# Dealing the weight products out among the attention slots: half a tile to a slot, or a whole tile to every second one

## What is computed

```
p  = project(modulate(rms_norm(x)), mix_w_in)
ya = diff_attend(...)       # 8 heads, two score maps each, p0 - lam * p1
yb = sink_attend(...)       # 16 query heads, window of 128 tokens, sink column
yc = mla_attend(...)        # 8 heads, scores from two parts (128 + 64 wide)
merged = ga * (ya @ branch_w[0]) + gb * (yb @ branch_w[1]) + gc * (yc @ branch_w[2])
```

## Time and profile before

| | us |
|---|---|
| median of three runs | 2768.34 |
| the runs | 2767.23 to 2771.36 |
| span of the profiled execution (one more execution) | 2769.1 |
| TensorE busy in it | 2694.7 (97%) |
| TensorE weight loads | 2257.3 (82%) |
| VectorE busy | 1745.0 (63%) |
| ScalarE busy | 1240.7 (45%) |
| GpSimd busy | 220.3 (8%) |

### The profile page before, as it was taken

One profiled execution on the slowest core, in us unless ns is written; L12 is line 12 of the kernel. 1 busy time (PEld: TensorE's weight loads), 2 busy tenths in 40 slices (PEclk: granted clock), 3 DMA queues, 4 the chain that ended last, 5 costly groups with the idle time before them and its releaser, 6 DMA issues.

```text
span 2769.1 us, 42026 instructions
## 1 busy us (share of the span) xinstructions
PE 2694.7 (97%) x15406; PEld 2257.3 (82%) x15406; DVE 1745.0 (63%) x2891; ACT 1240.7 (45%) x2212; POOL 220.3 (8%) x302
## 2 busy tenths in 40 slices
PE   8999999999999999999999999999999999998998
PEld 6888898886766776788888898888988777877996
DVE  6777366657755443358676385773667886646764
ACT  3222355227655444445222353222553576554543
POOL 0011010110100000010000000010102110000000
PEclk8999999999999999999999999999999999999999
DMA  7555357431111221145455455553555322424654
GB/s 277 181 188 194 102 163 242 130 106 39 47 46 39 73 91 39 54 160 184 160 195 163 119 174 183 189 193 109 157 189 175 122 77 70 127 83 152 230 179 152
DMA packets 105634, 384.42 MB, mean 139 GB/s; under 512 B 12049, under 2 KB 12321, under 8 KB 103569
## 3 DMA queue, kind: packets, MB, share of 16 engines
q1 hardware_dynamic: 85250, 303.34, 33.9%
q0 software_dynamic: 20240, 79.14, 8.8%
HBM read 379.27 MB, written 3.16 MB: 138 GB/s over the span
## 4 chain that ended last, share of the span: by engine, by line
PE 87%; DVE 8%; ACT 3%; DMA 1%; issue 1%; POOL 0%; SPq 0%; DVEq 0%; ACTq 0%; POOLq 0%
PE ps L2186 23%; PE ps L2194 22%; PE ps L2187 22%; PE ps L956 4%; PE ps L935 3%; PE ps L918 2%; DVE wlo L1613 2%; PE ps L2250 1%; PE ps L908 1%; PE ps L2252 1%; PE ps L2247 1%; PE ps L2126 1%; PE ps L2277 1%; PE ps L2274 1%; PE ps L2278 1%
## 5 line engine op out<-in xcount | busy, mean ns | idle before, releaser
L1613 DVE TENSOR_TENSOR wlo<-raw,whi 128x1024 fp32r<-128x1024 f32 x570 | 695.9, 1229 | 414.4 <-ACT whi L1233 413.3
L1233 ACT ACTIVATE whi<-raw 128x1024 fp32r<-128x1024 f32 x570 | 603.1, 1058 | 503.4 <-PE ps L2194 411.8
L2186 PE MATMUL ps<-xhi,whi 128*128 128x512 f32 (+1 forms) x2432 | 819.6, 351 | 6.5 <-DVE xlo L1804 5.3
L2187 PE MATMUL ps<-xlo,whi 128*128 128x512 f32 (+1 forms) x2432 | 812.1, 348 | 0.0
L2186 PEld LDWEIGHTS ps<-xhi,whi 128*128 128x128 f32 x2432 | 461.3, 190 | 71.0 <-DVE xlo L1804 6.5
L2187 PEld LDWEIGHTS ps<-xlo,whi 128*128 128x128 f32 x2432 | 461.6, 190 | 57.1
L2194 PE MATMUL ps<-xhi,wlo 128*128 128x512 f32 (+1 forms) x2432 | 505.1, 350 | 2.7 <-DVE wlo L1613 2.7
L2194 PEld LDWEIGHTS ps<-xhi,wlo 128*128 128x128 f32 x2432 | 399.2, 190 | 60.6 <-DVE wlo L1613 3.3
L1943 DVE SCALAR_TENSOR_TENSOR work<-ada,work 128x1024 f32<-128x1024 f32 x256 | 299.6, 1221 | 5.9 <-DMA ada<-in_ada_rows 5.9
L806 DVE TENSOR_REDUCE mx<-ps 128x2 f32<-128x1024 f32 (+1 forms) x120 | 125.2, 1045 | 185.6 <-PE ps L914 81.5
L2186 PE MATMUL ps<-ghi,whi 128*128 128x256 f32 (+1 forms) x792 | 233.5, 320 | 0.1
(11 more groups left out here) (253 smaller groups left out, 3438.7 us busy)
## 6 DMA issues: line engine op xcount, KB each, us to landing
raw<-in_ffn_in SPq DMA_DIRECT2D x192, 512.0 KB, 4.8
ada<-in_ada_rows POOLq DMA_DIRECT2D x128, 512.0 KB, 4.0
raw<-in_merge SPq DMA_DIRECT2D x96, 512.0 KB, 3.5
raw<-in_ffn_out SPq DMA_DIRECT2D x72, 512.0 KB, 3.6
raw<-in_v_a SPq DMA_DIRECT2D x32, 512.0 KB, 4.3
raw<-in_qk_a SPq DMA_DIRECT2D x32, 512.0 KB, 3.5
raw<-in_ffn_out SPq DMA_DIRECT2D x36, 384.0 KB, 3.2
raw<-in_out_rows SPq DMA_DIRECT2D x22, 512.0 KB, 3.5
```

The lines of the kernel that those rows point to most:

```text
L1233: act.activation(whi[:, g.ring(SPLIT), :], raw[:, g.ring(RAW), :], ACT.Copy).then_inc(hi_ready, 1)
L1613: dve.tensor_tensor(wlo[:, g.ring(SPLIT), :], raw[:, g.ring(RAW), :], whi[:, g.ring(SPLIT), :].bitcast(F32), ALU.subtract).then_inc(lo_rea ...
L2186: pe.matmul(o, w, hi[:, first + c, ph.span], start=start, stop=False)
L2187: pe.matmul(o, w, lo[:, first + c, ph.span], start=False, stop=False)
```

## The change

`share` rounds each cumulative number of ticks down to an even one. A slot then gets no product step or two, and a tile's high and low half stand in one slot, on TensorE, ScalarE, VectorE and GpSimd alike. Nothing is computed otherwise, no instruction is added or removed, and the number of ticks of a phase stays the same.

```diff
     parts = [3] + [1] * (2 * ph.steps)
     whole, so_far, out = sum(parts), 0, []
+    assert ticks % 2 == 0
     for part in parts:
         so_far += part
-        out.append(so_far * ticks // whole)
+        out.append(so_far * ticks // whole // 2 * 2)
     return out
```

## The result

The changed kernel takes 2800.74 us, the median of four runs (2797.33 to 2804.88), against 2768.16 (2767.23 to 2771.36) for the kernel before beside it: a ratio of 1.0113, 95% interval 1.0101 to 1.0125, 31 us slower. The forecast was 2792, in a range of 2774 to 2808. The profiled execution has a span of 2797.2 us. Lines of the changed kernel stand one further down: L935 is now L936, L918 is L919, L1233 is L1234.

What follows compares the result with a forecast made beforehand. TensorE, busy 97% of the span, was the engine to follow, with only 20.5 us of waits in the attentions. Terms 11.2 + 5.7 + 10 + 1.6 - 4.7 = +23.8 us gave 2792, range 2774 to 2808.

Steps and rivals of the forecast that it cites:

- The bound, and the place: Six attention windows, 690.8 us with 20.5 of waits: their sum grows by 24, and nothing moves outside them.
- Term 1: Attention starts: high halves that covered the first chain move away, leaving TensorE waiting; +11.2 us, bounds 8 and 12.
- Term 4: Starts of a0 and a1: idling about 3.0 us lowers TensorE's granted clock; one such cost, +1.6 us, bounds 0 and 5.
- Term 2: Modes b and c: steps left without product work make TensorE wait; +5.7 us, bounds 2 and 10.
- Term 3: Mode a: VectorE falls behind in longer stretches without products; +7 us in a0 and +3 in a1.
- Term 5: Attention units: 59 fewer entries into product work save 0.08 us each; -4.7 us, bounds -1.8 and -11.8.
- Nothing measurable: Rival: VectorE's leads cover mode a's stretches, starts cost 8, switches save 8; +5 us, 2773; chance 0.12.
- Faster by switches: Rival: each of 59 saved entries is worth 0.3 us, 17.7 in all; -5.7 us, 2762.6; chance 0.05.
- The others being the bound: Rival: ScalarE and VectorE bound the attentions, 41 added steps without products cost 0.7 each; +42 us, 2810; chance 0.12.

Runs made afterwards that it cites:

- starts kept: The changed kernel, but slots 0 to 3 of each attention keep the old list, whole tiles from slot 4 on: 2779.35 us, ratio 1.0037 to the kernel before.
- waits filled: The changed kernel with extra matmuls, results unused, in TensorE's waits at four attention starts (a0, b0, a1, b1): 2790.44 us, ratio 1.0079 to the kernel before.
- run 7: The changed kernel, with ScalarE, VectorE and GpSimd doing each tile's second step one slot later than TensorE, except latnorm's sums: 2805.45 us, ratio 1.0132.
- run 5: The kernel before, with only TensorE walking the new list (except latnorm's two sums), the other engines the old one: 2807.27 us, ratio 1.0148.
- run 2: The kernel before, but slots 0 to 3 of each attention have the new list, the old one behind: 2787.64 us, ratio 1.0070.
- run 11: The kernel before with extra matmuls, results unused, in two TensorE waits outside the attentions (8.9 and 3.0 us): 2766.20 us, ratio 0.9994.

## Why the prediction was right, step by step

**The bound, and the place.** Right: the six windows grew by 28.2 where 24 was forecast, and what moved outside them adds up to nothing.

**Term 1, the starts: +11.2.** Right in place and size. All waits stand where they were put: 3.0 us in a0, 0.9 grown to 3.0 in a1, 1.9 in b0, 1.0 grown to 2.9 in b1. The kernel after lies 21.0 above the run with its starts kept; less the 9.4 of the filled waits that is 11.6, give or take 5. The stages say it more finely: waits filled less starts kept is 3.1, 2.6, 1.2, 2.0 and 2.0 in a0, b0, c0, a1 and b1, where 3.6, 2.7, 0.8, 2.0 and 2.1 were forecast.

**Term 4, the clock: +1.6.** This is the term that was mis-sized. The step that failed is "I take one such cost": the same pause stands at every start that loses its half, and the text said itself that a0 and a1 would both idle for 3.0 us. The clock fell behind four starts, twice as long in a0, 8.5 us of lost clock in the profile, of which filling the waits returned 9.4 (give or take 5) in the medians and 5.9 in the touched stages. By the stages the stated bound of 5 was too low as well. Its other half, that slow matmuls partly fill waits, holds in part: 2.9 of 5.1 us of lost clock were paid in a0 and b0, 3.0 of 3.4 in a1 and b1.

**Term 2, steps in modes b and c: +5.7.** Right. With the starts kept, the windows of b0, c0, b1 and c1 hold 2.7, 0.8, 0.8 and 0.8 us more of waits than before, 5.1.

**Term 3, mode a: +10.** Half as large, and for another reason. With the starts kept a0 and a1 hold 2.8 and 2.7 more, 5.5. For a0 that is 0.2 us to each of 14 tiles, where 0.5 was forecast and below 0.2 was to count as a sign of being wrong. A lag of VectorE's would show as turns waiting for `prob` from VectorE, or as ScalarE waiting for maxima ahead of the scores' wait. The first fell in a0, from 1.1 to 0.7; the second is in neither of the two longer waits of scores behind a0's start (run 7). What grew is the scores behind ScalarE's `prob` (1.5 us in a0), the turns behind `back` (0.7 in a0, 1.1 in a1) and those behind GpSimd's scaling (0.6 and 0.4). Ahead of these scores stand ScalarE's copies of the tile, which the prediction had declared harmless. What delays `back` and the scaling was not taken apart by a run.

**Term 5, switches: -4.7.** Wrong. An entry's 0.11 us is in the record of the low half, but in sum TensorE's busy time moved by +0.3 with whole tiles and by +1.0 with twice the entries. The price of an entry can't be taken from one instruction's record. (The whole lists hold 71 fewer entries, not 59, which would have made the term larger still.)

**The sum.** Terms 2, 3 and 5 made 11.0 together, measured 10.2: the errors of 3 and 5, some 5 us each, cancelled, which is luck. What is left of 31.3 - 23.8 is the clock.

**What the prediction left out.** It saw ScalarE's split moving and found it covered by the tile's 5.4 us. Against run 5, which leaves the split where it was, this move is worth about 10 us (give or take 6).

**The rivals.** Nothing measurable needed the leads of mode a and the switches; the starts alone exclude it. Faster by switches needed 0.2 an entry. The others being the bound, +42, needed 34 us in the steps without products; with the starts kept the waits grew by 10.7.

## What to carry to other kernels

Independent work woven into a dependent chain is worth most in small pieces, as long as changing between the two costs little: here 48 matmuls in a lump cost 51.5 us, 24 cost 31, 8 at a time won 4, 4 at a time 14. Look first at the start and the tail of each chain, where a missing piece is lost in full, and reckon a pause of TensorE of 2 to 3 us as one that may be paid twice, for itself and for the clock behind it (1.7 or 3.4 us lost each time here, though not every time). When TensorE gets its work in larger lumps, look at the other engines' share of the same work: here moving it along was 10 us better than leaving it. In pieces smaller than before, it could stay where it was.

## What the runs showed of the hardware that was not expected

- In the kernel after the granted clock fell to 0.50 behind waits of TensorE of 3.00, 3.00 and 2.90 us, and in b0 behind one of 1.85. With matmuls of no use in the same places it stayed at 1.00. The length of the wait alone doesn't settle it: behind 2.89 us at the start of b1 it stayed at 1.00 in runs 2 and 5, and behind 2.12 us at the end of a0 it fell in run 2, where behind 2.13 before it did not. The Trainium skill ("TensorE: Matmul & The Clock Gate", HAM oscillation) warns of idle gaps of TensorE only from a length that none of these waits reaches; here the measurement decides.
- How far a kernel's runs differ goes largely with their mean clock: the run with the starts only took 2783.5 at 0.991 and 2791.5 at 0.987, the kernel after 2797.3 at 0.989 and 2804.9 at 0.987.
- Lost clock costs less time than it shows. Behind the attentions' starts TensorE's busy time was 7.5 us higher with 8.5 us lost (678.1 against 670.6 with the starts kept, run 1), and filling the waits gave 5.9 back in the stages. In the last stage 4.6 us less of it gave 2.4, as 2.0 of it had lain within the wait and a later wait took up part of the rest (run 11).
- Going to and fro between float32 turns and scores and the `F32R` products cost under 0.01 us a time, over 147 more entries.
